# The left-over count is loaded, and the branch over the general path marked, one expert group ahead of the branch

## The chip, the cores and the metric

One core of a Trainium2 chip (trn2) runs the whole program. The metric is the device time of one execution in microseconds; a shorter time is better. The kernel before takes 1652.74 us in the median of 3 runs (1652.52 to 1653.62).

## What is computed

The input is 256 tokens of 1024 features in float32. A first block adds three things to them in turn: a mixer (a bidirectional mLSTM beside a gated MLP over positions), cross attention to 256 memory rows, and a mixture of experts. A second block of two layers follows, each with a Hyena convolution, gated linear attention, a pooling branch and a feed-forward part. The part around the change is the mixture of experts, cut to its core:

```python
def hier_moe(h, w_rg, b_rg, w_re, b_re, w_gate, w_up, w_down):
    g_logits = (h @ w_rg) + b_rg                       # 4 groups, the best one is taken
    p_top, g_idx = lax.top_k(jax.nn.softmax(g_logits, axis=-1), 1)
    e_logits = take_along_axis(((h @ w_re) + b_re).reshape(T, 4, 8), g_idx)
    e_top, e_local = lax.top_k(e_logits, 2)            # 2 of its 8 experts
    weights = p_top * jax.nn.softmax(e_top, axis=-1)
    ...
    return (jax.nn.silu(xb @ w_gate[e]) * (xb @ w_up[e])) @ w_down[e]   # weighted and added up
```

## The kernel before

Five engines run programs of their own, written out by hand in order (`tensor_program`, `scalar_program`, `vector_program`, `gpsimd_program`, `sync_program`), and they meet at semaphores. `Port` (line 154) wraps an engine: it leaves out waits that were met already, and each engine's program is run once without an engine, to count semaphores.

**The experts.** The 32 experts are worked in `GROUPS` = 16 groups of two (g = 0 to 15). Each expert has 64 places (`CAP`): a token that chose it takes a place, and the tokens of a group are gathered into `XT` by one-hot matmuls. All of the weights come from `in_ws_dram` in units of 1 MB. A group has 12 units: 4 of the gate, 4 of the up and 4 of the down matrices. SyncE fetches them (`fetch`, line 627) into 19 homes on the chip: 7 slots of `RING` and 12 borrowed buffers whose names begin with e (`ew`, `ez`, ...). A home is filled again once TensorE has used its unit: `sync_experts` (line 2237) waits for unit v and then fetches the unit that follows it in its home. Units count from `U_MOE` = 33, so group 14 has units 201 to 212, group 15 has units 213 to 224, and the first units of the second block's layers are 225 to 231. The names stand in the order of their use: of units 213 to 224 the first two are in `ew` homes, the third in `ez`, the next four in `RING`, then `ew`, three in `RING`, `ew`.

For a group TensorE (`tensor_experts`, line 2273) does the 8 units of gate and up products into banks 0 and 1 (matmuls `P<-RING,XT` and `P<-ew,XT`), transposes of the hidden values (`P<-CONS,GS`), and the 4 units of down products (`P<-RING,HT`). ScalarE applies Silu and copies (`GS`, `HT`, `YSH`), VectorE multiplies (`GS`) and makes the low part `YSL`. The group's result is brought back to the tokens' order by the matmuls `P<-YSH,ST` and `P<-YSL,ST` (`tensor_combine`), and VectorE adds it to `X`. A group's combine is usually done during the next group; the one of group 14 is done at once, since the general path comes behind it.

**The general path.** A token whose expert has no place left is handled by `*_general` (line 2651 on): code that does all 32 experts for all tokens, with weights fetched anew. It is entered only when the largest number of tokens that chose one expert is over 64. `vector_experts` puts that number into `CNT` and raises the semaphore `count["ready"]` before the first group. Each engine then, at its own place between groups 14 and 15, waits for `ready` (met long ago), loads `CNT` into a register and branches. GpSimd does so near the start of its expert part. On TensorE the code that is branched over is 32 experts of 48 matmuls and 8 transposes each.

**After the experts** `tensor_between` (line 2850) combines group 15 and transposes `X`, and the first of the two layers begins with products of `rh_mix` and the high (`WH`) and low (`RINGL`) parts of units 225 on. `X<-X,SM,GF` is the first block's last norm, which uses the gains that SyncE loads into `GF` behind the last expert units.

Of the kernel before, what the change touches and what calls it, by code (L numbers as in the profile page):

```python
# [23 lines left out]
GROUPS = 16  # L24
# [129 lines left out]
class Port:  # L154
# [60 lines left out]
    def dma_start(self, *a):  # L215
        return self.engine.dma_start(*a) if self.engine else self

    @contextlib.contextmanager
    def overflow(self, count, most):

        met = dict(self.met)
        if self.engine is None:
            yield
        else:
            c = self.engine.value_load(count, min_val=0, max_val=512)
            with self.engine.If(c > most):
                yield
        self.met = met


# [4 lines left out]
CAP = 64  # L235
# [1958 lines left out]
def first_unit(g):  # L2194
    return U_MOE + g * UNITS_PER_GROUP
# [11 lines left out]
def filter_steps(steps, g):  # L2207

    n = g - FILTER_FIRST
    return [(n // 4, i) for i in steps[n % 4]] if 0 <= n < 8 else []  # L2210
# [26 lines left out]
def sync_experts(e, m, s, A):  # L2237
    e.wait_ge(*s.product["places"])
    e.wait_ge(*s.vec["places"])
    fetch(e, m, s, A, 51)  # L2240
    for v in range(U_MOE, U_B2):
        if v == first_unit(15):
            sync_general(e, m, s, A)
        if v in m.follow:
            e.wait_ge(*s.unit[v])
            fetch(e, m, s, A, m.follow[v])
        if v == first_unit(3):
            sync_tables(e, m, s, A)
            sync_filter(e, m, s, A, 0)
        if v == first_unit(8):  # L2250
            sync_filter(e, m, s, A, 1)
    e.dma_start(m.GF2[:, :], A["g_final"].partition_broadcast(128)).then_inc(*s.g_final_in.up(0))
# [20 lines left out]
def tensor_experts(e, m, s):  # L2273
    for step in (2, 3, 4, 5):
        tensor_prepare(e, m, s, 0, step)
    for g in range(GROUPS):
        for which in range(2):
            for kp in range(4):
                tensor_products(e, m, s, g, which, kp)

        for G, step in gather_steps(g):
            tensor_prepare(e, m, s, G, step)
        for t, n in combine_parts(g, False):
            tensor_combine_part(e, m, s, g - 1, t, n)
        b = m.next_misc(("hidden", g))
        e.wait_ge(*s.drain["hidden", g])
        for sig, event in m.free[b]:
            e.wait_ge(*sig[event])
        for k in range(4):
            p = e.transpose(m.P[b][:, k * 128:(k + 1) * 128], m.GS[:, k * 128:(k + 1) * 128], m.con("ident"))  # L2290
        p.then_inc(*s.turn.up("hidden", g))
        m.free[b] = [(s.evac, ("hidden", g))]

        for G, step in turn_steps(g):
            tensor_prepare(e, m, s, G, step)
        for t, n in combine_parts(g, True):
            tensor_combine_part(e, m, s, g - 1, t, n)
        for l, i in filter_steps(FILTER_PRODUCTS, g):
            tensor_filter(e, m, s, l, i)
        for k in range(4):  # L2300
            tensor_down(e, m, s, g, k)
        if g == GROUPS - 2:
            tensor_combine(e, m, s, g)
            tensor_general(e, m, s)
# [128 lines left out]
def scalar_experts(e, m, s):  # L2433
    e.preload_act_table_set("silu_and_others")
    for g in range(GROUPS):
        for l, i in filter_steps(FILTER_SINE, g - 1):
            scalar_filter(e, m, s, l, i)
        e.wait_ge(*s.unit[first_unit(g) + 3])
        if g:
            e.wait_ge(*s.turn["hidden", g - 1])  # L2440
        e.activation(m.GS[:, :], m.P[0][:, :], ACT.Silu).then_inc(*s.evac.up("silu", g))
        e.wait_ge(*s.turn["hidden", g])
        if g:
            e.wait_ge(*s.unit[first_unit(g) - 1])
        e.activation(m.HT[:, :, :], m.P[m.bank["hidden", g]][:, :].rearrange("p (k s) -> p k s", k=4),
                     ACT.Copy).then_inc(*s.evac.up("hidden", g))
        for G, step in turn_steps(g):
            scalar_prepare(e, m, s, G, step)
        for l, i in filter_steps(FILTER_PRODUCTS, g):
            scalar_filter(e, m, s, l, i)  # L2450
        e.wait_ge(*s.unit[first_unit(g) + 11])
        if g:
            e.wait_ge(*s.combined[g - 1, 1, 1])
        e.wait_ge(*s.evac["weights", g // 2, g % 2])
        for n in range(2):
            e.activation(m.YSH[:, n * 512:(n + 1) * 512], m.P[2 + n][:, :], ACT.Copy,
                         scale=slot_weight(m, g)).then_inc(*s.evac.up("y", g, n))
        if g == GROUPS - 2:
            scalar_general(e, m, s)
# [33 lines left out]


def gpsimd_experts(e, m, s):
    gpsimd_general(e, m, s)
    e.wait_ge(*s.evac["filter", 0, 1, 1])
    e.wait_ge(*s.combined[GROUPS - 2, 1, 1])
    e.tensor_copy(m.K0[:, :, :, :], m.K0W[:, :, :, :]).then_inc(*s.gained.up("filter"))
# [4 lines left out]
def vector_experts(e, m, s):  # L2504
    vector_prepare(e, m, s, 0, 1)
    most = route_row(m, 6, 1)
# [6 lines left out]
    vector_prepare(e, m, s, 0, 6)  # L2513
    vector_prepare(e, m, s, 1, 1)
    for g in range(GROUPS):
        G = g // 2 + 1
        for l, i in filter_steps(FILTER_EARLY, g - 1):
            vector_filter(e, m, s, l, i)
# [129 lines left out]

def sync_general(e, m, s, A):
    e.wait_ge(*s.count["ready"])
    with e.overflow(m.CNT[0:1, 0:1], CAP):
        e.wait_ge(*s.combined[GROUPS - 2, 1, 1])
        e.wait_ge(*s.evac["filter", 1, 1, 1])
        e.wait_ge(*s.gen_a["rows"])
        for ex in range(32):
            u = U_MOE + (ex // 2) * UNITS_PER_GROUP
            parts = A["ws"][u:u + 12].rearrange("k p (e c) -> p k e c", e=2)[:, :, ex % 2, :]
            for j in range(3):  # L2660
                if j or ex:
                    e.wait_ge(*s.gen_p["used", 3 * ex + j - 1])
                e.dma_start(m.WF[:, :, :], parts[:, 4 * j:4 * j + 4, :]).then_inc(*s.gen_in.up(3 * ex + j))
        e.wait_ge(*s.gen_v["out", 31])


def tensor_general(e, m, s):
    e.wait_ge(*s.count["ready"])
    with e.overflow(m.CNT[0:1, 0:1], CAP):
        e.wait_ge(*s.drain["moe", GROUPS - 2, 1, 1])  # L2670
        e.wait_ge(*s.gen_v["rows"])
        for k in range(8):
# [30 lines left out]


def scalar_general(e, m, s):
    e.wait_ge(*s.count["ready"])
    with e.overflow(m.CNT[0:1, 0:1], CAP):
        e.wait_ge(*s.gen_p["rows"])
        for k in range(8):
            p = e.activation(m.H32[:, k, :], m.P[k // 2][:, (k % 2) * 256:(k % 2) * 256 + 256], ACT.Copy, scale=m.par("g_moe", k))  # L2710
# [7 lines left out]


def gpsimd_general(e, m, s):  # L2720
    e.wait_ge(*s.count["ready"])
    with e.overflow(m.CNT[0:1, 0:1], CAP):
        e.wait_ge(*s.gen_v["out", 31])


def vector_general(e, m, s):
    e.wait_ge(*s.count["ready"])
    with e.overflow(m.CNT[0:1, 0:1], CAP):
        e.wait_ge(*s.combined[GROUPS - 2, 1, 1])
        e.wait_ge(*s.evac["filter", 1, 1, 1])  # L2730
        e.wait_ge(*s.gained["moe"])
# [3 lines left out]
        for ex in range(32):  # L2735
# [11 lines left out]
            for t in range(2):  # L2747
                for n in range(2):
                    v = m.X[:, t, n * 512:(n + 1) * 512]
# [1399 lines left out]
```

## Time and profile before

| what | value |
|---|---|
| median of 3 runs | 1652.74 us (1652.52 to 1653.62) |
| the profiled execution | 1651.14 us |
| its span, first to last instruction | 1649.3 us |
| mean granted clock of TensorE | 0.992 |
| TensorE busy | 1590.3 us, 96% of the span |
| VectorE, ScalarE, GpSimd busy | 940.6, 730.8 and 94.3 us |
| moved by DMA | 399.82 MB, mean 242 GB/s |

The profile is of one execution. PE is TensorE's matmuls and PEld its weight loads; a q behind an engine's name means its sequencer, which waits, branches, loads registers and issues DMAs while the engine itself may still be busy or idle. Register and branch instructions are not counted as busy. Of an instruction the profile gives the line of the code, the operation and its tiles (out<-in). The span is 1.84 us shorter than the same execution's time, and that execution is 1.6 us shorter than the median of the runs.

### The profile page before, as it was taken

To read this page: it belongs to the slowest core of one execution; us is meant where nothing else is said; L and a number is where in the kernel's file an instruction comes from. 1 tells how busy PE (TensorE), PEld (TensorE's weight loads), DVE (VectorE), ACT (ScalarE), POOL (GpSimd) and SP (SyncE) were. 2 spreads that over 40 slices of the span, in tenths; PEclk is the share of its full clock that TensorE was granted. 3 is DMA by queue.
4 is the path that set the end of the run, shared out by engine and by line. 5 is a ranking of instruction groups with operands and counts; after the bars stand their busy time and mean duration, and the time that the engine had idled before them with its cause. 6 is when DMAs were issued, how large, how long until landed. Compare 5 with 4: busy or idle time off the path is not lost.

```text
span 1649.3 us, 22868 instructions
## 1 busy us (share of the span) xinstructions
PE 1590.3 (96%) x9309; PEld 1199.4 (73%) x9309; DVE 940.6 (57%) x1600; ACT 730.8 (44%) x1391; POOL 94.3 (6%) x83
## 2 busy tenths in 40 slices
PE   7999997999999999789999999999999999999998
PEld 6997884444334334239997889999789978889997
DVE  5967655222332332237675567766767756677665
ACT  6755542101110010036663447655666643575554
POOL 1010001000000000014001000000230010000000
PEclk9999998999999999999999999999999999999999
DMA  9434577999999999984344445555444444545550
GB/s 358 176 128 145 200 283 286 378 393 424 423 424 403 424 424 424 423 364 175 133 169 163 166 155 192 190 191 180 162 157 150 168 165 157 185 168 181 187 195 26
DMA packets 57414, 399.82 MB, mean 242 GB/s; under 512 B 6612, under 2 KB 7029, under 8 KB 9946
## 3 DMA queue, kind: packets, MB, share of 16 engines
q1 hardware_dynamic: 57306, 398.32, 62.5%
q8 instruction: 75, 1.23, 0.3%
q14 instruction: 33, 0.27, 0.1%
HBM read 397.24 MB, written 1.05 MB: 241 GB/s over the span
## 4 chain that ended last, share of the span: by engine, by line
PE 85%; DMA 9%; DVE 3%; ACT 1%; issue 1%; SPq 0%; DVEq 0%
PE P L171 83%; DMA RING<-in_ws_dram 7%; PE P L174 2%; DMA ez<-in_ws_dram 1%; DMA W<-in_hw_dram 1%; DVE RINGL L183 1%; DVE X L189 0%; ACT WH L177 0%; DVE SM L189 0%; DVE rl_mix L189 0%; ACT JNK L177 0%; DVE YB L183 0%; ACT L180 0%; DVE RT L189 0%; DVE HS L189 0%
## 5 line engine op out<-in xcount | busy, mean ns | idle before, releaser
L183 DVE TENSOR_TENSOR RINGL<-RING,WH 128x1024 fp32r<-128x1024 f32 x338 | 419.9, 1275 | 131.0 <-ACT WH L177 129.8
L177 ACT ACTIVATE WH<-RING 128x1024 fp32r<-128x1024 f32 x351 | 358.2, 1055 | 53.7 <-PE P L171 50.7
L171 PE MATMUL P<-HA,WH 128*128 128x256 f32 x1208 | 345.1, 286 | 0.0
L171 PE MATMUL P<-LA,WH 128*128 128x256 f32 x1208 | 340.3, 282 | 0.0
L171 PE MATMUL P<-HA,RINGL 128*128 128x256 f32 x1208 | 340.3, 282 | 0.0
L171 PEld LDWEIGHTS P<-HA,WH 128*128 128x128 f32 x1208 | 227.7, 189 | 5.8 <-issue 3.0
L171 PEld LDWEIGHTS P<-HA,RINGL 128*128 128x128 f32 x1208 | 228.3, 189 | 2.1
L171 PEld LDWEIGHTS P<-LA,WH 128*128 128x128 f32 x1208 | 228.6, 189 | 0.0
L171 PE MATMUL P<-RING,XT 128*64 128x512 f32 x632 | 143.5, 595 | 7.0 <-DMA RING<-in_ws_dram 7.0
L171 PEld LDWEIGHTS P<-RING,XT 128*64 128x64 f32 x632 | 44.2, 137 | 101.6 <-issue 79.7
L183 DVE TENSOR_TENSOR GS<-P,GS 128x512 f32<-128x512 f32 x16 | 11.1, 692 | 180.2 <-PE P L171 180.2
L171 PE MATMUL P<-WH,HA 128*128 128x512 f32 x272 | 110.6, 407 | 1.3 <-ACT VN L177 1.3
L171 PE MATMUL P<-RINGL,HA 128*128 128x512 f32 x272 | 107.5, 395 | 1.8 <-POOL RINGL L183 1.6
L171 PE MATMUL P<-WH,LA 128*128 128x512 f32 x272 | 107.1, 394 | 0.0
L189 DVE SCALAR_TENSOR_TENSOR YSL<-P,SM,YSH 128x512 fp32r<-128x512 f32 x32 | 22.6, 746 | 125.8 <-ACT YSH L177 125.8
L177 ACT ACTIVATE YSH<-P,SM 128x512 fp32r<-128x512 f32 x32 | 20.3, 684 | 139.7 <-PE P L171 139.7
L177 ACT ACTIVATE HT<-P 128x512 f32<-128x512 f32 x16 | 9.6, 598 | 151.6 <-PE P L174 151.6
L189 DVE SCALAR_TENSOR_TENSOR CVT<-QPC,PARS,CVT 128x256 f32<-128x256 f32 x104 | 53.5, 515 | 36.0 <-ACT CVT L177 33.9
L171 PE MATMUL P<-WH,FL 128*128 128x512 f32 x176 | 69.8, 397 | 0.0
L171 PE MATMUL P<-RINGL,FH 128*128 128x512 f32 x176 | 69.4, 394 | 0.0
L171 PE MATMUL P<-WH,FH 128*128 128x512 f32 x176 | 69.3, 394 | 0.0
L177 ACT ACTIVATE QPC<-P 128x256 f32<-128x256 f32 x68 | 26.0, 382 | 85.9 <-PE P L171 85.9
(403 smaller groups left out, 2689.8 us busy)
## 6 DMA issues: line engine op xcount, KB each, us to landing
RING<-in_ws_dram SPq DMA_DIRECT2D x288, 1024.0 KB, 5.0
ew<-in_ws_dram SPq DMA_DIRECT2D x47, 1024.0 KB, 20.8
ez<-in_ws_dram SPq DMA_DIRECT2D x16, 1024.0 KB, 19.8
ek<-in_ws_dram SPq DMA_DIRECT2D x6, 1024.0 KB, 10.4
ef<-in_ws_dram SPq DMA_DIRECT2D x4, 1024.0 KB, 10.7
eha<-in_ws_dram SPq DMA_DIRECT2D x2, 1024.0 KB, 4.8
ela<-in_ws_dram SPq DMA_DIRECT2D x2, 1024.0 KB, 6.6
TAB<-in_dft_dram SPq DMA_DIRECT2D x2, 1024.0 KB, 5.6
```

The source lines that it names most:

```text
L171: return self.engine.matmul(*a, **k) if self.engine else self
L174: return self.engine.transpose(*a) if self.engine else self
L177: return self.engine.activation(*a, **k) if self.engine else self
L183: return self.engine.tensor_tensor(*a) if self.engine else self
L189: return self.engine.scalar_tensor_tensor(*a) if self.engine else self
```

## The change

Each engine's wait for `ready` and its load of `CNT` move to a new function, `watch_count`, which is called at the start of group 14 (on GpSimd directly ahead of the branch, as there is no loop there). Behind the load the place is marked, and the branch later refers to the mark. The branch itself is written out with `br_cond`: to `fits_...` when the count is under 65, else to `over_...`, the general path, which ends in a branch to `fits_...`. Before, `If(c > 64)` made these blocks.

```diff
+    def watch(self, count):
+        if self.engine:
+            self.count = self.engine.value_load(count, min_val=0, max_val=512)
+            self.seen = self.engine.mark_branch_hint_location()
+
     @contextlib.contextmanager
-    def overflow(self, count, most):
+    def overflow(self, most):
 
         met = dict(self.met)
         if self.engine is None:
             yield
         else:
-            c = self.engine.value_load(count, min_val=0, max_val=512)
-            with self.engine.If(c > most):
+            name = str(self.engine.engine).split(".")[-1]
+            self.engine.br_cond(self.count < most + 1, f"fits_{name}", f"over_{name}").branch_hint(self.seen)
+            with self.engine.bass.body(f"over_{name}", valid_engines=[self.engine.engine]):
                 yield
+                self.engine.br(f"fits_{name}")
+            self.engine.bass.switch_bb(f"fits_{name}")
         self.met = met
...
 def tensor_experts(e, m, s):
...
     for g in range(GROUPS):
+        if g == GROUPS - 2:
+            watch_count(e, m, s)
...
+def watch_count(e, m, s):
+    e.wait_ge(*s.count["ready"])
+    e.watch(m.CNT[0:1, 0:1])
+
...
 def tensor_general(e, m, s):
-    e.wait_ge(*s.count["ready"])
-    with e.overflow(m.CNT[0:1, 0:1], CAP):
+    with e.overflow(CAP):
         e.wait_ge(*s.drain["moe", GROUPS - 2, 1, 1])
```

The same two edits are made for the other engines: `scalar_experts` and `vector_experts` call `watch_count` at `g == GROUPS - 2`, `sync_experts` at unit 201, `gpsimd_experts` directly ahead of `gpsimd_general`.

On TensorE the order of the program changes at two places, the start of group 14 and the end of its combine. The first piece of the difference is the start of group 14 (HT are the down products of group 13, XT the gate products of group 14, each row 4 matmuls per unit); rows with + are the changed kernel's.

```order
 L171 MATMUL P<-ew_201,HT 64x512 x4
 L171 MATMUL P<-RING,HT 64x512 x8
+L221 TENSOR_LOAD CNT
+L221 ISA x2
+L222 BRANCH_PREFETCH_HINT
 L171 MATMUL P<-RING,XT 64x512 x4
 L171 MATMUL P<-ew_202,XT 64x512 x4
```

The load, its two register instructions and one new instruction, the mark, now stand between the last unit of group 13 and the first of group 14. The second piece is the branch itself, behind the combine of group 14; below it the general path begins.

```order
 L171 MATMUL P<-YSH,ST 128x512
 L171 MATMUL P<-YSL,ST 128x512
-L225 TENSOR_LOAD CNT
-L225 ISA x2
-L226 COMPARE_AND_BRANCH
+L232 COMPARE_AND_BRANCH
 L174 MATMUL P<-CONS,XN_130 128x128 x16
 L171 MATMUL P<-WF,H_131 128x512 x32
```

Only the branch is left there. The general path itself, and everything behind it, keeps its order.

## Rows read from the trace of the kernel before

**Rows 1.** The page: the span, busy times and the chain by engine.
```profile
span 1649.3 us, 22868 instructions
PE 1590.3 (96%) x9309; PEld 1199.4 (73%) x9309; DVE 940.6 (57%) x1600; ACT 730.8 (44%) x1391; POOL 94.3 (6%) x83
PE 85%; DMA 9%; DVE 3%; ACT 1%; issue 1%; SPq 0%; DVEq 0%
```
**Rows 2.** Lines L226 and L225: duration ns min/median/max, first and last start.
```profile
L226 ACTq COMPARE_BRANCH  x1: 45/45/45, 692.5 to 692.5; - x1
L226 PEldq COMPARE_BRANCH  x1: 6180/6180/6180, 694.8 to 694.8; - x1
L226 DVEq COMPARE_BRANCH  x1: 72/72/72, 696.3 to 696.3; - x1
...
L225 PEldq TENSOR_LOAD <-CNT x1: 491/491/491, 694.0 to 694.0; - x1
L225 PEldq FUSED_REGOPS  x1: 165/165/165, 694.5 to 694.5; - x1
```
**Rows 3.** The chain that ended last, at the branch: start, duration, what.
```profile
695.39 5.69 issue
```
**Rows 4.** Timeline of PE behind the branch: start, duration, instructions, idle before.
```profile
701.08 5.91 PE L171 MATMUL P<-ew,XT 128*64 128x512 f32 x16 [5.69 <-issue]
706.82 1.88 PE L171 MATMUL P<-ez,XT 128*64 128x512 f32 x8
708.54 7.03 PE L171 MATMUL P<-RING,XT 128*64 128x512 f32 x32
715.40 1.88 PE L171 MATMUL P<-ew,XT 128*64 128x512 f32 x8
...
719.59 5.37 PE L171 MATMUL P<-RING,HT 128*64 128x512 f32 x24 [0.78 <-ACT HT L177]
724.76 1.92 PE L171 MATMUL P<-ew,HT 128*64 128x512 f32 x8
```
**Rows 5.** Windows: busy of PE, PEld, DVE, ACT, POOL; granted clock, DMA share, GB/s.
```profile
695.00:701.00 6.00, 0.39 (x2) 0.00 (x0) 1.39 (x3) 0.00 (x0) 1.89 (x1) 0.82 1.01 416
701.00:706.00 5.00, 4.92 (x14) 1.52 (x16) 0.00 (x0) 0.00 (x0) 0.00 (x0) 0.53 1.01 415
```
**Rows 6.** DMA queues: the whole span, 668 to 670 us, and 698 to 700 us.
```profile
q8 instruction: 75, 1.23, 0.3%
...
q8 instruction: 1, 0.02, 3.2%
...
q8 instruction: 1, 0.02, 3.4%
```
**Rows 7.** Timeline of PE in group 14, and the last unit's wait.
```profile
666.00 3.60 PE L171 MATMUL P<-ew,XT 128*64 128x512 f32 x16
669.94 1.94 PE L171 MATMUL P<-ez,XT 128*64 128x512 f32 x8 [0.34 <-DMA ez<-in_ws_dram]
672.42 1.94 PE L171 MATMUL P<-RING,XT 128*64 128x512 f32 x8 [0.54 <-DMA RING<-in_ws_dram]
...
689.73 1.94 PE L171 MATMUL P<-RING,HT 128*64 128x512 f32 x8 [0.16 <-DMA RING<-in_ws_dram]
```
**Rows 8.** DMA issues from 704 and from 725.3 us: KB, us to landing; their start.
```profile
ew<-in_ws_dram SPq DMA_DIRECT2D x1, 1024.0 KB, 14.4
GF<-in_g_final_dram SPq DMA_DIRECT2D x1, 512.0 KB, 13.2
...
704.80 0.34 SPq L216 DMA_DIRECT2D ew<-in_ws_dram  x1
```
**Rows 9.** Timelines of ACT and DVE: first uses of units 225 on, and of GF.
```profile
733.21 3.94 ACT L177 ACTIVATE WH<-RING 128x1024 fp32r<-128x1024 f32 x4
745.57 2.74 DVE L189 SCALAR_TENSOR_TENSOR X<-X,SM,GF 128x512 f32<-128x512 f32 x4
```
**Rows 10.** Waits of PEld from 742 us to the end: total, times, longest.
```profile
PEld P L174 <- DVE X L189: 5.7, 3, 2.3
```

More of the change, by code:

```diff
@@ L2241, in sync_experts @@
     for v in range(U_MOE, U_B2):
+        if v == first_unit(14):
+            watch_count(e, m, s)
         if v == first_unit(15):
@@ L2276, in tensor_experts @@
     for g in range(GROUPS):
+        if g == GROUPS - 2:
+            watch_count(e, m, s)
         for which in range(2):
@@ L2435, in scalar_experts @@
     for g in range(GROUPS):
+        if g == GROUPS - 2:
+            watch_count(e, m, s)
         for l, i in filter_steps(FILTER_SINE, g - 1):
@@ L2495, in gpsimd_experts @@
 def gpsimd_experts(e, m, s):
+    watch_count(e, m, s)
     gpsimd_general(e, m, s)
@@ L2515, in vector_experts @@
     for g in range(GROUPS):
+        if g == GROUPS - 2:
+            watch_count(e, m, s)
         G = g // 2 + 1
@@ L2667, in tensor_general @@
 def tensor_general(e, m, s):
-    e.wait_ge(*s.count["ready"])
-    with e.overflow(m.CNT[0:1, 0:1], CAP):
+    with e.overflow(CAP):
         e.wait_ge(*s.drain["moe", GROUPS - 2, 1, 1])
@@ L2705, in scalar_general @@
 def scalar_general(e, m, s):
-    e.wait_ge(*s.count["ready"])
-    with e.overflow(m.CNT[0:1, 0:1], CAP):
+    with e.overflow(CAP):
         e.wait_ge(*s.gen_p["rows"])
@@ L2720, in gpsimd_general @@
 def gpsimd_general(e, m, s):
-    e.wait_ge(*s.count["ready"])
-    with e.overflow(m.CNT[0:1, 0:1], CAP):
+    with e.overflow(CAP):
         e.wait_ge(*s.gen_v["out", 31])
 def vector_general(e, m, s):
-    e.wait_ge(*s.count["ready"])
-    with e.overflow(m.CNT[0:1, 0:1], CAP):
+    with e.overflow(CAP):
         e.wait_ge(*s.combined[GROUPS - 2, 1, 1])
```

## The prediction

> **What bounds the kernel now.** I began with the page. TensorE is busy for 96% of the span and carries 85% of the chain that ended last; DMA carries 9%, and 1% is "issue", time in which TensorE waited for nothing that the profile shows [rows 1]. A branch can only be worth something in that last part, so I asked for the branch's own line. It stands between groups 14 and 15. On ScalarE and VectorE it takes 45 and 72 ns; on TensorE it takes 6180 ns [rows 2]. The chain has the same place from the other side: TensorE's combine ends at 695.39 us and 5.69 us of "issue" follow [rows 3]; the first unit of group 15 starts at 701.08 [rows 4]. All five programs do the same compare; what sets TensorE apart is the code that it jumps over, by far the longest.
>
> What the branch waits for stands in the DMA view. The instruction queue q8 moved 1.23 MB in 75 packets, 16 KB each, and TensorE ran 9309 matmuls and as many weight loads [rows 1, 6], so one packet holds about 250 of its instructions. That is one every 22 us in the mean. One falls at 668 to 670 us; the views of the queue up to 694 list no other; the next falls at 698 to 700 us, behind the branch's start at 694.8, and TensorE goes on just behind it, at 701.08. I read the 6.18 us as the time to fetch the code at the branch's target.
>
> The stall costs more than its length: the granted clock is 0.82 over the idle stretch and 0.53, the lower level of 1.2 GHz, in the 5 us behind it [rows 5]. The first 16 matmuls there take 5.91 us; 16 of the same form in group 14 take 3.60 [rows 4, 7]. That is 2.3 us more.
>
> The second bound here is the weights. In group 14 TensorE waits for units: they start at 669.94 and 672.42 us, each ended by a DMA, and the last one at 689.73 [rows 7]. These are units 204, 205 and 212, so a unit lands every 2.48 us (1 MB, 424 GB/s), while TensorE needs 1.72 us for one (706.82 to 708.54). During the stall the DMA engines run on at full share [rows 5]; units pile up, and afterwards TensorE runs group 15 without a single wait for a DMA [rows 4].
>
> **The change, part by part.**
>
> *The branch on TensorE.* If the mark has the target's code fetched in advance, the branch should cost what it costs elsewhere, 45 to 72 ns, and that lies under the last combine matmuls, as the load did before: the branch began at 694.8 and the matmuls end at 695.39. I take 0. The upper bound is that all 6.18 us stay. The 5.69 us of idle time and the 2.3 us of slow clock go: 8.0 us on TensorE alone.
>
> *What is late next: the weights.* Without the stall, unit 213 starts at about 695.3 us and group 15 runs at 1.72 us a unit, into the landings. The last unit of the group, 224, is the one that decides. It was issued at 704.80 and landed 14.4 us later, at 719.2 [rows 8]. The cadence says the same: 689.7 + 12 x 2.48 = 719.4. An earlier issue does not land it sooner, since the queue is full and in order (DMA share 1.01 throughout, rows 5). Is another unit later? Unit 220 (the last of gate and up) lands at 719.2 - 4 x 2.48 = 709.3. From its start to the first down unit it takes 719.59 - 715.40 = 4.2 us (VectorE's product, transposes, ScalarE's copy), so the down units start at 713.5, 715.2 and 717.0, and unit 224 could start at 718.7. It waits half a microsecond for its landing, until 719.3. In the kernel before it starts at 724.76 [rows 4]. **The gain at this point is 5.5 us**, not 8.0: 2.5 us of it are given to the weights.
>
> *Does it last?* Behind unit 224 all work moves up by 5.5 us unless something lands too late. Units 225, 226 and 227 land at 721.7, 724.2 and 726.7 by the cadence; ScalarE's run of four casts (two of unit 226, two of 227, one microsecond each) began at 733.21 [rows 9] and would begin at 727.7, the third of them at 729.7. GF was issued at 725.36, about when unit 223 was done, and landed 13.2 us later [rows 8], at 738.6; its first use moves from 745.57 [rows 9] to 740.1. That fits with 1.5 us to spare. From 742 us to the end TensorE's list of waits has no DMA in it, and its longest wait is 2.3 us, for VectorE [rows 10]: that part is its own work and moves as a block. I take 5.5 us through to the end; the bounds are 4.0 (GF or a cast is late by its margin) and 5.7 (all of the idle time).
>
> *The load, moved, and the mark.* The load and its register operation take 0.49 + 0.17 = 0.66 us of TensorE's sequencer [rows 2]. They went under the combine before; now they stand ahead of unit 201, which began one unit before the row at 666.00, at 664.3 [rows 7]. The mark is not in this trace; between the cheap compares and the load it costs 0.05 to 0.49 us [rows 2], and I take the lower, as it only sets the sequencer, like them without a tile. Even with all of it exposed, up to 1.15 us, TensorE is then behind at 664 and meets its waits for landings at 669.94 (0.34 us), 672.42 (0.54 us) and at the units after [rows 7]: the delay is gone by unit 206. Price 0; without that cover, 0.7 to 1.2 us. On SyncE the load delays one fetch by as much; even behind the stall, at 704.80, the queue holds 14.4 us of work [rows 8], so 0. On ScalarE and VectorE a group's work is a few operations in some 27 us, and the load falls between them; 0. GpSimd branches where it did.
>
> The sum: 1649.3 - 5.5 = 1643.8 us of span, 1645.6 with the 1.84 us around it. Against the median of the runs, 1652.74, I forecast **1647.2 us**.
>
> **A rule weighed.** Row and rule agree that such a jump is expensive. The rows also bear on whether the mark can help. It stands about 235 instructions ahead of the branch (32 matmuls of 64x512 in two passes, and 20 smaller ones, with their weight loads), just less than one packet's 250, and is run at 662 to 664 us, 4 us or more ahead of the packet at 668 to 670. So the mark comes ahead of the last packet that the straight run asks for. The Trainium skill (Runtime: NRT & Kernel Launch, Instruction fetch mechanics) says that prefetch is purely sequential and that a taken branch outside the window has to fetch. By that, the mark would do nothing and the sum would be 1652.7. No row here has a mark in it, so the trace cannot tell; its mechanism is the first rival.
>
> **The rivals.**
>
> *1. The mark does nothing*: packets come in line or at a miss, and in no other way. TensorE's branch stays at about 6.2 us and all else too; the load's move is hidden. For it: the trace shows packets only in a straight run and at the miss. Against it: the mark names the target some 30 us ahead, and in all that time only one packet is to be brought. Time 1652.7. Chance 0.13.
>
> *2. The weights do not bind after all*, and the full 8.0 us are kept. For it: with TensorE idle less, nothing. Against it: the landing at 719.2. Time 1644.7. Chance 0.03.
>
> *3. Part of it is given back* where the experts end: GF or the casts are late by more than I reckon, or TensorE's clock falls where it now waits half a microsecond per unit. Against it: such waits stand in the groups before too, and the mean granted clock is 0.992. Time 1648.7 to 1650. Chance 0.05.
>
> *4. Slower: the target's packet takes the place of the next one in line.* Between 670 us and the branch TensorE runs nearly a packet of code. If the straight-line code crosses into a new packet between the mark and the branch, and the mark has sent the fetcher elsewhere, TensorE stalls there for about 6.2 us; and if the target's code is dropped for it, it stalls again at the branch. The first stall is largely absorbed by the weights, as now; the second then comes on top, with nothing left to absorb it, and 6.2 us are added: 1658.9. It decides if the crossing lies ahead of the branch. Against it: in the kernel before no packet falls between 670 and 694, and the one at 698 comes with the branch, so the code up to the branch was there already. Chance 0.04.
>
> **How the numbers follow.** The forecast, 1647.2, has a chance of 0.75; its own range is 1646.2 to 1648.7, from the bounds 4.0 and 5.7 and half a microsecond of spread between medians. A measurement of this kernel can tell about 0.2%, 3.3 us, from no change, so the border of "faster" is 1649.4. Faster holds the forecast, rival 2 and over half of rival 3, 0.81; the same holds rival 1 and the rest of 3, 0.15; slower is rival 4, 0.04. The range runs from 1645.8 to 1650.0 and leaves out rivals 1, 2 and 4, together 0.20.
>
> **What would show it.** In the changed kernel's profile: the compare on TensorE under 0.2 us; an instruction packet for it around 665 to 670 and none at 698; no "issue" of microseconds near 695; the granted clock at 1.00 from 695 to 706; TensorE waiting for DMAs in group 15, and unit 224 starting at 719.3. I am wrong if the compare still takes 6 us (rival 1), if unit 224 starts before 718 (rival 2), or if it starts at 719.3 and the end is not 5.5 us earlier (rival 3).

## The result, and the profile after

The changed kernel takes 1648.51 us in the median of 8 runs (1646.25 to 1651.15), against 1652.87 us for the kernel before in 8 runs (1652.46 to 1654.98; the 3 of the prediction are among them). The ratio is 0.9974, with a 95% interval of 0.9966 to 0.9983: faster by 4.4 us, about 0.3%, where 5.5 us were forecast. The profiled execution took 1646.75 us, with a span of 1644.9 us and a mean granted clock of 0.992.

The page of the changed kernel, the lines that answer to [rows 1] and the first of [rows 6]:

```profile
span 1644.9 us, 22873 instructions
...
q8 instruction: 74, 1.21, 0.3%
...
PE 83%; DMA 12%; DVE 3%; ACT 1%; issue 0%; POOL 0%; SPq 0%; DVEq 0%
```

The 1% of "issue" is gone from the chain, DMA has risen from 9 to 12%, and the instruction queue brought one packet fewer. The branch's line is now L232, the load's L221 and the mark's L222. Columns as in [rows 2]:

```profile
L232 ACTq COMPARE_BRANCH  x1: 68/68/68, 692.6 to 692.6; - x1
L232 PEldq COMPARE_BRANCH  x1: 401/401/401, 694.9 to 694.9; - x1
L232 DVEq COMPARE_BRANCH  x1: 84/84/84, 696.4 to 696.4; - x1
...
L222 PEldq BRANCH_PREFETCH_HINT  x1: 55/55/55, 660.9 to 660.9; - x1
```

The compare on TensorE fell from 6180 to 401 ns. The mark is an instruction of its own and takes 55 ns. The compares of ScalarE and VectorE became a little dearer, 68 and 84 ns for 45 and 72.

The chain that ended last, at the branch and behind it, where [rows 3] had 5.69 us of "issue":

```profile
694.23 3.98 PE P L171 x15
...
698.22 21.98 DMA ew<-in_ws_dram
...
720.24 1.96 PE P L171 x8
```

Now the chain leaves TensorE at 698 us for a fetch of weights, and comes back with its landing. The timeline of PE behind the branch, which answers to [rows 4]:

```profile
696.24 3.65 PE L171 MATMUL P<-ew,XT 128*64 128x512 f32 x16
699.73 1.89 PE L171 MATMUL P<-ez,XT 128*64 128x512 f32 x8
701.45 3.60 PE L171 MATMUL P<-RING,XT 128*64 128x512 f32 x16
705.46 1.94 PE L171 MATMUL P<-RING,XT 128*64 128x512 f32 x8 [0.41 <-DMA RING<-in_ws_dram]
707.92 1.94 PE L171 MATMUL P<-RING,XT 128*64 128x512 f32 x8 [0.52 <-DMA RING<-in_ws_dram]
710.37 1.94 PE L171 MATMUL P<-ew,XT 128*64 128x512 f32 x8 [0.51 <-DMA ew<-in_ws_dram]
...
714.60 5.37 PE L171 MATMUL P<-RING,HT 128*64 128x512 f32 x24 [0.78 <-ACT HT L177]
720.24 1.94 PE L171 MATMUL P<-ew,HT 128*64 128x512 f32 x8 [0.27 <-DMA ew<-in_ws_dram]
```

Unit 213 starts at 696.24 instead of 701.08, and its 16 matmuls take 3.65 us instead of 5.91. From the sixth unit on (705.46) TensorE waits for landings of gate and up units, and unit 224 starts at 720.24 us, as soon as its weights are there, instead of 724.76. The windows, which answer to [rows 5], show why the 16 matmuls are short: the granted clock stays at the upper level, 1.00, where it had been 0.82 and 0.53.

```profile
695.00:701.00 6.00, 6.00 (x27) 2.38 (x29) 2.31 (x4) 0.00 (x0) 1.89 (x1) 1.00 1.02 416
701.00:706.00 5.00, 4.59 (x24) 1.40 (x22) 0.00 (x0) 0.60 (x1) 0.00 (x0) 1.00 1.01 421
```

The instruction queue in two windows of 1 us, 668 to 669 and 698 to 699 us, and a long one, 700 to 712 us, in that order (packets, MB, share of 16 engines):

```profile
q8 instruction: 1, 0.02, 6.3%
...
q8 instruction: 1, 0.02, 6.4%
...
q1 hardware_dynamic: 693, 5.05, 101.0%
q14 instruction: 2, 0.02, 0.3%
```

There are packets at 668.5 and 698.5, as before. The kernel before had a third one at 704.2 us, right behind the stall; here no q8 row stands between 700 and 712. The trace doesn't say what a packet holds. I infer that the packet at 668.5, which the kernel before has too, now brings the branch's target, and that the one at 698.5 is the piece of code behind it, which the kernel before fetched at 704.2.

What follows moved as a block. The run of four casts begins at 728.72 (733.21 in [rows 9]) and the first use of GF at 741.09 (745.57), both 4.5 us earlier:

```profile
728.72 3.95 ACT L177 ACTIVATE WH<-RING 128x1024 fp32r<-128x1024 f32 x4
...
741.09 2.74 DVE L189 SCALAR_TENSOR_TENSOR X<-X,SM,GF 128x512 f32<-128x512 f32 x4
```

From unit 224's start to the end of the span it is 924.7 us in this profile, and 924.5 in that of before. The whole difference between these two executions is made by then.

### The profile page after: what moved, and what is told of

It reads as the page before. It is cut to its first block, busy times and chain, and to the rows that moved or that the text cites. A ratio compares the mean times of both kernels' runs of the same rounds, so it can differ in the third digit from the quotient of the medians.

```text
span 1644.9 us, 22873 instructions
## 1 busy us (share of the span) xinstructions
PE 1589.9 (97%) x9309; PEld 1199.0 (73%) x9309; DVE 940.5 (57%) x1600; ACT 730.8 (44%) x1391; POOL 94.2 (6%) x83
## 4 chain that ended last, share of the span: by engine, by line
PE 83%; DMA 12%; DVE 3%; ACT 1%; issue 0%; POOL 0%; SPq 0%; DVEq 0%
PE P L171 81%; DMA RING<-in_ws_dram 8%; PE P L174 2%; DMA ew<-in_ws_dram 1%; DMA W<-in_hw_dram 1%; DMA ez<-in_ws_dram 1%; DVE RINGL L183 1%; DVE X L189 0%; ACT WH L177 0%; DVE SM L189 0%; DVE rl_mix L189 0%; ACT JNK L177 0%; DVE YB L183 0%; ACT L180 0%; DVE RT L189 0%
```

## The experiments

Three questions were open. Is it the mark, or the load that moved with it? Are the weights the second bound? And what does the mark do? The last also asks how far ahead it has to stand, and whether my fourth rival (the target's code displaces other code) exists at all. Twelve runs were made. All are edits of the changed kernel, except that one starts from the kernel before and one is the changed kernel itself; a ratio is always to the kernel before on the same chip.

### The load moved, without the mark

```diff
-            self.seen = self.engine.mark_branch_hint_location()
...
-            self.engine.br_cond(...).branch_hint(self.seen)
+            self.engine.br_cond(...)
```

> The changed kernel without the marks: the load stays ahead of group 14 on all engines, the branch has no mark. Theory M (the mark alone brings the code of the branch's target in advance): TensorE's compare is back at about 6.2 us, a code packet falls at 698 and a second one at 704, unit 224 starts at about 724.8, and the time is that of before, 1652.9 us (within 0.5). Theory L (the gain comes from the load being out of the way, or from the way the two blocks are written out): the compare stays at 0.4 us and the time stays near 1648.5.

Measured: 1651.84 us (1650.49 to 1654.28, 10 runs), before 1653.05 (24 runs), ratio 0.9994 (0.9984 to 1.0004). The compare takes 6028 ns again. The branch's line:

```profile
L231 PEldq COMPARE_BRANCH  x1: 6028/6028/6028, 694.4 to 694.4; - x1
```

The timeline of PE, the first and the last unit of group 15:

```profile
700.46 5.05 PE L171 MATMUL P<-ew,XT 128*64 128x512 f32 x16 [4.67 <-issue]
...
723.29 1.92 PE L171 MATMUL P<-ew,HT 128*64 128x512 f32 x8
```

Without the mark the stall is back, and the gain with it. But the idle time is 4.67 us, not 5.69. The compare begins 1.4 us before TensorE runs out of matmuls (694.4 against 695.79); in the kernel before it began 0.55 us before, since there the load and its register operation stand directly ahead of it (0.66 us, [rows 2]). As long as the branch stalls, moving the load is a gain of its own, about 1 us of idle time, that I had put at 0.

### The mark and the moved load on TensorE alone

TensorE keeps its call of `watch_count` at the start of group 14, with the mark; the other engines make it directly ahead of their branch, without one.

```diff
-def watch_count(e, m, s):
+def watch_count(e, m, s, mark=False):
...
-            self.seen = self.engine.mark_branch_hint_location()
+            self.seen = self.engine.mark_branch_hint_location() if mark else None
```

> The kernel before with the load and the mark moved on TensorE alone; ScalarE, VectorE, SyncE and GpSimd load directly ahead of their branches and have no mark. Theory M: only TensorE's branch had anything to gain, so the compare takes 0.4 us and the time is that of the changed kernel, 1646.5 to 1650. Theory E (every engine's mark counts, the other four give a part of the gain): the time lies between, 1650 to 1652.

Measured: 1648.59 us (1647.16 to 1650.22, 9 runs), ratio 0.9973 (0.9963 to 0.9983), the compare on TensorE 397 ns. As far as the times can tell, all of the gain comes from this one engine. The compares of VectorE and ScalarE are back at 72 and 45 ns: the 12 and 23 ns more are what a marked branch costs there.

### Half of the weights of group 15, with and without the stall

Here the fetches of units 213 to 224 bring half of each unit, so that the queue has half as much to move for them. The rest of a buffer keeps what was there.

```diff
+    if U_MOE + 15 * UNITS_PER_GROUP <= u < U_B2:
+        e.dma_start(m.slot[m.home[u]][:, 0:1024], A["ws"][u][:, 0:1024])...
```

In the kernel before:

> The kernel before, with only the first half of each of the units 213 to 224 fetched (512 KB less each, 6.3 MB less in all; the other half of these weights isn't loaded, so this leaves out part of the data). Unit 224 lands up to 14.8 us earlier. Theory W (in the kernel before, TensorE runs group 15 behind landings that were long there; in the changed one unit 224's landing is what it waits for): no change from before, 1652.9 within 0.7, unit 224 starts at 724.8. Theory N (the weights have no part in it in either kernel): no change either. Should it be faster by over 2 us, then the weights bind behind group 15 as well, which neither expects.

In the changed kernel:

> The changed kernel with the same halved fetches of units 213 to 224 (leaves out the same part of the data). Theory W: TensorE runs group 15 without waits, unit 224 starts at about 716.8 and the gain against before is the full 5.7 us of idle time and 2.3 us of slow clock, 8.0 us: 1644.9 (within 0.7), and the runs lie as close together as those of before, within about 1 us. Theory N (something else than unit 224's landing takes the 3.6 us between 8.0 and the measured 4.4): the time stays at 1648.5, spread over 5 us as the changed kernel's.

Measured: 1652.84 us in the kernel before (1649.98 to 1655.77, 10 runs), ratio 0.9998 (0.9989 to 1.0008); 1645.10 us in the changed one (1643.07 to 1646.29, 4 runs), ratio 0.9952 (0.9935 to 0.9968). The timeline of PE in the changed one, the fourth to seventh unit of group 15 (216 to 219) and the last (224):

```profile
701.79 7.04 PE L171 MATMUL P<-RING,XT 128*64 128x512 f32 x32
...
718.02 1.92 PE L171 MATMUL P<-ew,HT 128*64 128x512 f32 x8
```

No wait for a DMA is left in group 15. Lighter weights buy nothing while the branch stalls, and some 3 us more once it doesn't (1645.10 against 1648.51 for the changed kernel). That is step two of the prediction: freed of the weights, the marked branch is worth 7.7 us (1652.84 less 1645.10, both with half weights), and with whole weights 4.4 of them are left. The interval of the changed one is wide, with 4 runs, and their spread of 3.2 us is not the 1 us that I had expected. Unit 224's start came later than expected in both profiles, at 727.07 and 718.02 us for 724.8 and 716.8. In the first the stream itself ran late: unit 212 had landed at 692.60, 2.9 us behind its landing in before.

### The mark directly ahead of the branch

The load stays at the start of group 14. `mark` is a new method that holds the one line with `mark_branch_hint_location`; it is used in the runs below too.

```diff
             tensor_combine(e, m, s, g)
+            e.mark()
             tensor_general(e, m, s)
```

> The changed kernel with the marks (of all engines) directly ahead of the branches, the loads where the change has them; on TensorE the mark runs some 34 us later than in the changed kernel. Theory Q (the mark itself asks for the target's code at once): it comes 0.1 us before the branch, so the compare takes 6.0 to 6.2 us. Theory R (the mark only says which code the next regular packet is to bring): no regular packet lies between mark and branch, so 6.2 us as well. Both: time 1652.9. If the compare takes 0.4 us, both are wrong.

Measured in a single run: 1651.61 us, before 1653.23 (19 runs). Only TensorE's mark is at its branch, not those of all engines as the expectation says: ScalarE's still runs at 667.1 us. TensorE's runs at 695.86 us, the compare takes 6033 ns, "issue" is 4.79 us. A mark without lead did no good here, and one run shows no cost of it either.

### The mark 11 us ahead, behind the last packet before the branch

```diff
+        if g == GROUPS - 2:
+            e.mark()
         for k in range(4):
             tensor_down(e, m, s, g, k)
```

> The changed kernel with TensorE's mark behind the gate and up units of group 14, ahead of its four down units: about 9 to 10 us ahead of the branch, and behind the regular code packet at 668.5. A fetch took 6.2 us at the miss. Theory Q (the mark asks at once): a packet at about 688, compare 0.4 us, time 1648.5. Theory R (it redirects only the regular packet, which has already gone): no packet before the branch, compare 6.2 us, packets at 698 and 704, time 1652.9.

Measured: 1648.01 us (1646.11 to 1649.07, 8 runs), ratio 0.9970 (0.9960 to 0.9981), the whole gain. The lines of the branch and the mark:

```profile
L238 PEldq COMPARE_BRANCH  x1: 495/495/495, 695.7 to 695.7; - x1
...
L228 PEldq BRANCH_PREFETCH_HINT  x1: 55/55/55, 684.7 to 684.7; - x1
```

The instruction queue from 689 to 690 us; from 672 to 688 it has no row:

```profile
q8 instruction: 1, 0.02, 6.8%
```

The packet at 689.2 us stands in no other profile so far: it comes 4.5 us behind the mark, out of turn. The packet at 670.1 had already brought code before the mark was run, and the mark fetched its target by itself. So it doesn't only steer a packet that is due anyway. That a packet out of turn stands between mark and branch exactly where the stall is missing is the evidence that this packet holds the target.

### The mark a group earlier still, at group 13

```diff
+        if g == GROUPS - 3:
+            e.mark()
```

> The changed kernel with TensorE's mark at the start of group 13, some 55 us and about 460 of TensorE's instructions ahead of the branch, so that two regular code packets (638.7 and 668.5) fall between. Theory R1 (the mark redirects the packet that is asked for while the branch's own piece of code runs): works as in the changed kernel, compare 0.4 us, 1648.5. Theory R2 (it redirects the very next packet): the packet at 638.7 brings the target, TensorE misses its own next code near 665 and stalls there for about 6 us, and the branch is then cheap or not; that stall is largely absorbed by the weights: 1648.5 to 1653, and the trace shows a gap of about 6 us of issue near 665.

Measured: 1647.44 us (1645.61 to 1649.70, 6 runs), ratio 0.9966 (0.9953 to 0.9978). The mark runs at 634.0 us, 62 us ahead of the branch; the compare takes 398 ns. The instruction queue, 636 to 645 us, then 660 to 700:

```profile
q8 instruction: 1, 0.02, 0.7%
...
q8 instruction: 2, 0.03, 0.3%
```

The packets are at 640.6, 670.6 and 699.6 us: nothing out of turn, and no stall where straight-line code crosses into the next piece. TensorE's code went on without a stall, so I infer that the packet at 640.6 held straight-line code and that the mark was kept over it. My fourth rival, a mark that costs a stall because it sends the fetcher elsewhere too soon, did not happen even at nearly twice the distance.

### No branch on TensorE at all

The general path is left out of TensorE's program; it is never entered on this data.

```diff
-        if self.engine:
+        if self.engine and "PE" not in str(self.engine.engine):
...
         if self.engine is None:
             yield
+        elif "PE" in str(self.engine.engine):
+            kept, self.engine = self.engine, None
+            yield
+            self.engine = kept
```

> The changed kernel with neither load, mark nor branch on TensorE and without its code of the general path (this leaves out TensorE's part of the general path, which these inputs don't enter). Theory W: nothing is left to gain from the branch, since unit 224's landing ends the wait: 1646.5 to 1650, as the changed kernel. Theory C (the 0.4 us of the compare and what the code lengths do to the fetches still cost something): 0.4 to 1 us faster than the changed kernel.

Measured: 1647.96 us (1645.23 to 1649.09, 10 runs), ratio 0.9971 (0.9960 to 0.9981), unit 224 at 720.77. The same as with the marked branch, as far as the times can tell. The 0.40 us that the marked compare still takes, a good deal over the 0.2 that I had allowed, cost nothing: they lie under the last combine matmuls.

### The mark 4.2 us ahead

```diff
         for k in range(4):
             tensor_down(e, m, s, g, k)
         if g == GROUPS - 2:
+            e.mark()
             tensor_combine(e, m, s, g)
```

> The changed kernel with TensorE's mark moved from the top of group 14 to behind the group's down products, ahead of the call that combines the outputs, about 3 us before the branch; the other engines keep theirs. If a mark inside the branch's own piece of code asks for the target at once: an extra packet of the instruction queue at the mark, a compare of about 6.2 less the lead, so 2 to 4 us, and what is left of the stall lies under the weights that unit 224 waits for, so that it starts within 1 us of the marked kernels and the time is 1647.5 to 1649.5 us. If a mark that is late by less than the fetch is lost: a compare of 6.0 us, unit 224 past 723 and a time of 1651.5 to 1653 us. If every microsecond of a stall costs even here: 1650 to 1651 us.

Measured: 1651.57 us (1650.07 to 1653.37, 10 runs), before 1652.17 (19 runs), ratio 0.9996 (0.9986 to 1.0005). I had expected the leftover of the stall to be short; all of it is there.

The lines of the branch and the mark, then the timeline of PE, the first and the last unit of group 15:

```profile
L238 PEldq COMPARE_BRANCH  x1: 5913/5913/5913, 693.8 to 693.8; - x1
...
L228 PEldq BRANCH_PREFETCH_HINT  x1: 55/55/55, 689.6 to 689.6; - x1
```

```profile
699.76 6.19 PE L171 MATMUL P<-ew,XT 128*64 128x512 f32 x16 [4.56 <-issue]
...
723.72 1.92 PE L171 MATMUL P<-ew,HT 128*64 128x512 f32 x8
```

There is no q8 packet from 684 to 697 us; the first comes at 697.2, 3.4 us behind the branch, the second at 703.1. At 4.2 us ahead the mark wasn't worth a part of the fetch; it was worth nothing.

### The mark one unit earlier, twice

```diff
         for k in range(4):
+            if g == GROUPS - 2 and k == 3:
+                e.mark()
             tensor_down(e, m, s, g, k)
```

> The changed kernel with TensorE's mark one down unit earlier than in the run that marked behind them: ahead of the last of group 14's four, some 6 us before the branch instead of 4.2. The mark 4.2 us ahead bought nothing (compare 5913 ns, no packet between mark and branch), the one 11 us ahead did all, with its packet 4.5 us behind the mark. Theory A: a mark's packet comes 4.5 us behind it, and a branch that comes sooner asks for its target anew: then here a packet some 4.5 us behind the mark, a compare of 0.4 to 1.5 us, unit 224 at 720 to 722 and 1647.5 to 1649 us. Theory B: a mark must stand further ahead, by code or by time: no packet between, a compare near 6 us, unit 224 past 723, 1651.5 to 1653 us.

> The kernel of the run before once more, unaltered. Its ten times lay from 1644.89 to 1653.88 us, wider than any other's, with a median of 1651.4, though its profile showed the mark working: packet 3.4 us behind the mark, compare 495 ns, unit 224 at 720.04. Theory: the mark 6.7 us ahead of the branch is at the edge, and an execution either gets its target (near 1646 to 1648 us) or fetches it at the branch (1651 to 1653 us); then the times here again fall on both sides, and a profile of an execution on the dear side has no packet between mark and branch and a compare of about 6 us. Rival: the width is chance, the mark works in every execution: a median of 1647 to 1649 us like the other marked kernels.

Measured: 1651.41 us (1644.89 to 1653.88, 10 runs), ratio 0.9989 (0.9977 to 1.0001), and the same kernel again 1650.59 us (1646.33 to 1654.50, 12 runs), ratio 0.9988 (0.9978 to 0.9998). The two profiles show opposite things. The first, its lines of the branch and the mark:

```profile
L238 PEldq COMPARE_BRANCH  x1: 495/495/495, 694.7 to 694.7; - x1
...
L228 PEldq BRANCH_PREFETCH_HINT  x1: 55/55/55, 688.0 to 688.0; - x1
```

Its instruction queue from 691 to 692 us:

```profile
q8 instruction: 1, 0.02, 6.5%
```

Its timeline of PE, unit 224:

```profile
720.04 1.94 PE L171 MATMUL P<-ew,HT 128*64 128x512 f32 x8 [0.28 <-DMA ew<-in_ws_dram]
```

The second, the same lines, and the timeline of PE at units 213 and 224:

```profile
L238 PEldq COMPARE_BRANCH  x1: 6012/6012/6012, 695.8 to 695.8; - x1
...
L228 PEldq BRANCH_PREFETCH_HINT  x1: 55/55/55, 689.1 to 689.1; - x1
```

```profile
701.85 5.66 PE L171 MATMUL P<-ew,XT 128*64 128x512 f32 x16 [4.66 <-issue]
...
725.28 1.92 PE L171 MATMUL P<-ew,HT 128*64 128x512 f32 x8
```

In both the mark stands 6.7 us ahead of the branch. Once its packet came at 691.4 us and the compare was cheap; once none came until 699.3 and the stall was whole. The program is the same to the instruction, but these two executions ran on different chips, so the profiles alone could mean that the chip decides. The times within a series speak for each execution: of the first ten, all on one chip, three lie below 1650 and four above 1652; of the second twelve, five and two. The other kernels with the load moved and a stall in their profile never came below 1650.07 us, the changed kernel and the variants whose mark worked in their profile never above 1651.15. No profile shows both outcomes on one chip, so this is likely, not shown. A profile of one execution would have misled me here in either direction. What decides at 6.7 us stays open: neither the mark's distance to the branch (6.70 and 6.72 us) nor its distance to the last regular packet (19.4 and 18.9 us) tells the two apart, and at 21.6 us behind that packet and 4.2 ahead of the branch it failed.

### The changed kernel again

> The changed kernel once more, unaltered, beside the others on one chip, for a second profile of it. Theory that the size was off because one profile of before was at the dear end: 1648 to 1649 us again, with unit 224's start 29.5 to 31 us behind unit 212's landing, against 33 to 35 us in the unmarked ones. Rival, that the first profile of the changed kernel had a late stream by something the mark does: the same gap near 700 us of 0.8 us or more in the weight queue in this profile too, at the same place.

Measured: 1648.37 us (1647.36 to 1650.59, 10 runs), before 1652.17, ratio 0.9978 (0.9968 to 0.9988).

Unit 224 starts at 721.57, 29.6 us behind unit 212's landing, just as in the first profile of this kernel. The landings are read from the chain, as start and duration of the fetch. The rows of before and of this profile:

```profile
666.22 23.47 DMA RING<-in_ws_dram
...
668.46 23.52 DMA RING<-in_ws_dram
```

The 1.42 us wait at 670.88 us that the first one showed in group 14 is 0.36 here; it was that execution's own. The gap of the rival doesn't show in either profile: in windows of 1 us from 694 to 708 the DMA share is never under 0.96.

One thing is new. This span is 2.1 us longer than the first profile's. Of these, 1.4 had come by unit 212's landing (691.98 against 690.61), and 0.7 lie behind unit 224: 925.4 us to the end, where the first had 924.7. In the window from 730 to 740 us the granted clock is 0.83, where before and the first profile have 1.00:

```profile
730.00:740.00 10.00, 8.56 (x35) 6.96 (x35) 10.00 (x17) 8.60 (x21) 5.76 (x5) 0.83 0.89 358
```

## Why the prediction was right, and where its size was off

All profiles can be put on one scale: from the landing of unit 212, where the weight stream and TensorE meet ahead of the branch, to the start of unit 224, where they meet again. That takes out how late the stream ran by then.

| kernel | mark ahead of the branch, us | compare, ns | idle, us | first 16 matmuls, us | unit 212 lands to unit 224 starts, us |
|---|---|---|---|---|---|
| before | - | 6180 | 5.69 | 5.91 | 35.1 |
| before, half weights | - | 6017 | 5.52 | 5.47 | 34.5 |
| load moved, no mark | - | 6028 | 4.67 | 5.05 | 33.2 |
| mark at the branch | 0.1 | 6033 | 4.79 | 5.35 | 33.6 |
| mark ahead of the combine | 4.2 | 5913 | 4.56 | 6.19 | 34.2 |
| mark ahead of the last unit, second | 6.7 | 6012 | 4.66 | 5.66 | 33.8 |
| mark ahead of the last unit, first | 6.7 | 495 | 0 | 3.65 | 29.6 |
| mark ahead of the down units | 11.0 | 495 | 0 | 3.65 | 29.7 |
| the changed kernel | 34.0 | 401 | 0 | 3.65 | 29.6 |
| the changed kernel again | 33.0 | 398 | 0 | 3.65 | 29.6 |
| TensorE alone | 33.2 | 397 | 0 | 3.65 | 31.0 |
| mark at group 13 | 62.0 | 398 | 0 | 3.65 | 30.4 |
| no branch | - | - | 0 | 3.65 | 29.6 |
| the changed kernel, half weights | 33.8 | 397 | 0 | 3.65 | 27.1 |

*The compare is a fetch of the target's code: right.* With a mark that works it falls to 0.40 to 0.50 us, and the packet behind the stall is gone or has come earlier. What a packet holds is inferred from this, not seen. In the stalled profiles the packet comes 3.4 to 3.7 us into the compare; what fills the 2.5 us or so behind it the traces don't show. My bound of under 0.2 us was wrong, by a quantity that costs nothing. A marked branch on TensorE is not as cheap as on the other engines. I looked for the target's packet at 665 to 670 us, and one is there, at 668.5, but the kernel before has that one too; the sign is the missing packet at 704.2. That none would follow at 698 was wrong: one does, and I take it for the next piece of code. That TensorE stalls because it jumps over by far the longest code stays an argument: no run changes that length. VectorE jumps over 32 times 8 operations and two more, and its unmarked compare takes 72 ns.

*Why the mark could help: the argument was not needed.* The prediction set store by the mark coming ahead of the last packet of the straight run. In the kernel with its mark 11 us ahead it came behind that packet (684.7 against 670.1 us) and worked all the same. The distance of about 235 instructions holds, but not what stands behind it in brackets: a group has 48 matmuls of 64x512 in two passes, not 32 (96 + 20 with their weight loads are 232).

*The first rival, the rule that was weighed, fell.* The Trainium skill (Runtime: NRT & Kernel Launch, Instruction fetch mechanics) says that a taken branch out of the window fetches and stalls. In each of the six profiled executions without a working mark the trace agrees, with 5.9 to 6.2 us. That prefetch is purely sequential, as it also says there, does not hold for a marked branch: the packet at 689.2 us of the kernel with its mark ahead of the down units came out of turn.

*The slow clock goes with the stall: right.* From 695 to 706 us the granted clock was 1.00 in all profiles with a working mark or no branch.

*The weights take a part back: right.* Unit 224 decided, and it did wait for its landing. With half of the weights the changed kernel needs 27.1 us on the table's scale, with all of them 29.6: the weights hold 2.5 us, as forecast. By the times it is 3.4, and with 4 runs on one side that doesn't contradict it.

*The size of the stall: this step was off.* "The 5.69 us of idle time and the 2.3 us of slow clock go: 8.0 us on TensorE alone" came from one execution, and on the table's scale it is the dearest of the six with a stall. Against the one profile of its successor the step was right almost to the decimal: 35.1 - 29.6 = 5.5 us. That the two profiled spans differ by 4.4 us, like the medians, is chance: unit 212 landed 0.9 us later in the second (690.61 against 689.69). The six stalled executions have a mean of 34.1, the seven with no stall and whole weights one of 29.9, and 4.1 us lie between them. The length of the slow clock differs from one execution to the next: the first 16 matmuls took 5.05 to 6.19 us, 1.4 to 2.5 more than 3.65. And in some the stream itself runs late behind unit 212, as in the run on TensorE alone, 31.0. The 4.1 us agree with the medians, 4.4 and 3.8 us in the two series of the changed kernel. The 5.5 was the price of one execution, read as the mean.

*The moved load: 0 is right with a mark that works, and was wrong without one.* The two stalled profiles with the load at the branch have 5.69 and 5.52 us idle, the four with the load moved 4.56 to 4.79: the load made the compare start late by some 0.9 us. With a mark that works no idle time is left at the branch, and the weights decide. The kernel without a mark was 1.2 us faster than before by its median, which its interval can't tell from no change. This also explains a part of the mean of 34.1 above: 34.8 for the two with the load at the branch, 33.7 for the other four. Against the former the gain is 4.8 us (34.77 less 29.93), within what the series leave open.

*Does it last: right in these two profiles, not quite in all.* The 924.5 and 924.7 us behind unit 224 held in before and after, as did the casts and GF. But over all profiles with whole weights this stretch takes 924.5 to 925.9 us, with a mean of 924.9 in the five with a stall and 925.2 in the seven without. It is longest in the changed kernel again, in TensorE alone and with the mark at group 13 (925.4, 925.8 and 925.8), all three with a granted clock of 0.83 from 730 to 740 us, but also in the kernel without a mark (925.9), at the same clock; the one with its mark at the branch has that clock too, and 924.6. So nothing ties it to the mark. The prediction had no term for it; it takes some 0.3 us in the mean.

*Rivals two to four.* The full 8.0 us were kept only where the weights were halved (1645.10 us measured, against 1644.9 of the sum). The third, that part is given back where the experts end, is seen in three profiles with a working mark, at 0.7 to 1.1 us over the first. They have the lower clock there; that the clock alone costs this isn't shown. No mark, at 34 or 62 us, displaced code in line.

None of the variants beats the changed kernel by more than the measurement can tell: 1647.44 to 1648.59 us for those whose mark worked in their profile or that have no branch, against 1648.51. The mark stands well where it does. The only faster one is short of weights, which says what binds now: the stream of 1 MB each 2.48 us.

## What to carry to other kernels

A single compare of microseconds, where its sisters on other engines take tens of nanoseconds, was here the fetch of the target's code. A mark that names the target removed it: 11 us or more ahead of the branch it did so in each profile, while 6.7 us ahead it did so in one of two, and 4.2 us ahead not at all. Put it far ahead: even at 62 us no cost was seen. Price a stall from more than one execution, ask which stream has been catching up while it lasts, and move loads out from between the last work and the branch, since the stall runs from the moment the compare starts.

## What the runs showed that I had not expected

- A mark that is too late is lost whole. At 4.2 us ahead, no packet came until 3.4 us behind the branch, about the lag it has with no mark at all (3.7 us in before). The working late marks had their packets 3.4 and 4.5 us behind them.
- One and the same program, with its mark 6.7 us ahead, took the stall in one profiled execution and not in the other, and its times spread over 9.0 and 8.2 us, against 3.2 and 4.9 for the changed kernel (and up to 6.0 in 19 runs of before).
- An early mark seems to fetch nothing at once. At group 13 the next packet came 6.6 us behind it, in its turn, and another 30 us later. Which packet holds the target is inferred from the stalls that are missing; the trace doesn't say what a packet holds.
- With its target fetched in time, the branch still takes 0.40 us on TensorE with an early mark and 0.50 with a late one, and on ScalarE and VectorE a marked compare takes 68 and 84 ns, an unmarked one 45 and 72.
- The granted clock was 0.83 from 730 to 740 us in some profiles of stalled and of unstalled kernels, with up to 1.4 us more between unit 224 and the end; what decides it stays open.
- Behind a stall of nearly the same length TensorE's clock was at its lower level for different times. The granted clock from 695 to 701 and 701 to 706 us was 0.91 and 0.77 without the mark, where the kernel before had 0.82 and 0.53:

```profile
695.00:701.00 6.00, 1.33 (x6) 0.61 (x6) 1.79 (x3) 0.00 (x0) 1.89 (x1) 0.91 1.01 415
701.00:706.00 5.00, 5.00 (x20) 1.54 (x18) 0.00 (x0) 0.00 (x0) 0.00 (x0) 0.77 1.02 418
```
